# Output projection of layer 0 ended in passes over 256 and 320 tokens, with two tiles' norm beside the second pass

## What is computed

```python
def rms_norm(x, w):
    y = xf * lax.rsqrt(jnp.mean(xf * xf, axis=-1, keepdims=True) + NORM_EPS)
    return (y * w.astype(jnp.float32)).astype(x.dtype)

def diff_attn_output(o, g, subln_w, w_out):
    of = head_rms_norm(o) * subln_w * (1.0 - LAMBDA_INIT)
    gated = of.reshape(b, s, DA_WIDTH) * jax.nn.silu(g)
    return gated @ w_out

for layer in range(DEPTH):
    hp = rms_norm(y_prompt, norm_pre)
    ...
    y_prompt = y_prompt + rms_norm(diff_attn_output(op, gp, ...), norm_post)
```

## Time and profile before

| | |
|---|---|
| time, 3 runs | 3826.13, **3837.47** (median), 3842.16 us |
| profiled execution, its own time | 3831.26 us |
| its span and mean granted clock | 3828.5 us, 0.993 |
| PE busy | 3709.1 us (97%), 26980 matmuls |
| DVE, ACT, POOL busy | 1453.5 (38%), 1123.9 (29%), 150.6 (4%) us |
| DMA queue of loads | 565.92 MB, 47.6% of 16 engines' span |
| chain that ended last | PE 50%, then DVE 2%, each other 1% or less |

### The profile page before, as it was taken

The page is one execution under the profiler, slowest core; times in us unless marked ns, Lnnn a source line. Parts: engine busy times, 40 slices in busy tenths (PEclk is TensorE's granted clock), DMA queues, the critical chain, the costliest instruction groups (busy, mean ns, idle before and its releaser), DMA issues.

```text
span 3828.5 us, 70107 instructions
## 1 busy us (share of the span) xinstructions
PE 3709.1 (97%) x26980; PEld 3275.7 (86%) x26980; DVE 1453.5 (38%) x2215; ACT 1123.9 (29%) x1808; POOL 150.6 (4%) x87
## 2 busy tenths in 40 slices
PE   7999999999999999989899999999999999999998
PEld 7987887888788877767898989999989899989998
DVE  4244334433443344323633333333333324243345
ACT  4233233323332333221422222222222222232223
POOL 1000000200020002002200000000000000000000
PEclk9999999999999999999999999999999999999999
DMA  5456778687768776764442525242424343443333
GB/s 172 151 177 188 239 239 237 212 244 236 238 210 245 238 237 215 244 197 168 135 139 83 165 83 166 79 164 85 160 86 161 94 149 98 163 138 130 108 122 121
DMA packets 472204, 642.91 MB, mean 168 GB/s; under 512 B 35649, under 2 KB 294850, under 8 KB 468738
## 3 DMA queue, kind: packets, MB, share of 16 engines
q1 hardware_dynamic: 407122, 565.92, 47.6%
q10 hardware_dynamic: 64336, 72.24, 5.6%
q0 software_dynamic: 416, 0.28, 0.1%
HBM read 566.09 MB, written 70.65 MB: 166 GB/s over the span
## 4 chain that ended last, share of the span: by engine, by line
PE 50%; DVE 2%; issue 1%; DMA 1%; ACT 1%; POOL 1%; SPq 1%; ACTq 0%; DVEq 0%; POOLq 0%
PE low_banks L965 42%; PE high_banks L965 6%; PE high_banks L968 1%; DMA area<-in_cache_v 1%; POOL area L1897 1%; DVE WL L1523 0%; ACT WH L1236 0%; DMA WR<-in_w_in_ret 0%; SPq L900 0%; SPq L901 0%; ACTq L1401 0%; DVE area L1782 0%; ACT area L1236 0%; DVE area L1545 0%; ACTq L1400 0%
## 5 line engine op out<-in xcount | busy, mean ns | idle before, releaser
L965 PE MATMUL low_banks<-XH,WH 128*128 128x288 f32 (+2 forms) x6656 | 1545.6, 310 | 42.0 <-DVE XL L1528 16.6
L965 PE MATMUL low_banks<-XH,WL 128*128 128x288 f32 (+2 forms) x6656 | 1455.4, 296 | 0.0
L965 PE MATMUL low_banks<-XL,WH 128*128 128x288 f32 (+2 forms) x6656 | 1452.6, 296 | 0.0
L965 PEld LDWEIGHTS low_banks<-XH,WH 128*128 128x128 f32 x6656 | 1080.4, 190 | 142.4 <-issue 96.0
L965 PEld LDWEIGHTS low_banks<-XH,WL 128*128 128x128 f32 x6656 | 1083.7, 189 | 0.0
L965 PEld LDWEIGHTS low_banks<-XL,WH 128*128 128x128 f32 x6656 | 1083.4, 189 | 0.0
L1523 DVE TENSOR_TENSOR WL<-WR,WH 128x1024 fp32r<-128x1024 f32 x436 | 533.4, 1223 | 817.8 <-ACT WH L1236 812.7
L1236 ACT ACTIVATE WH<-WR 128x1024 fp32r<-128x1024 f32 x436 | 461.2, 1058 | 923.4 <-PE low_banks L965 652.6
L965 PE MATMUL high_banks<-area 128*32 128x512 f32 (+8 forms) x3696 | 654.1, 547 | 16.1 <-DVE area L1554 5.6
L1236 ACT ACTIVATE area<-high_banks 128x512 f32<-128x512 f32 x480 | 270.2, 569 | 1139.4 <-PE high_banks L968 756.8
L968 PEld LDWEIGHTS high_banks<-eye_sb,area 128*128 128x128 f32 (+2 forms) x3080 | 352.4, 142 | 156.6 <-issue 116.8
(11 more groups left out here) (113 smaller groups left out, 840.9 us busy)
## 6 DMA issues: line engine op xcount, KB each, us to landing
area<-in_cache_k SPq DMA_DIRECT2D x512, 256.0 KB, 4.1
area<-in_cache_v SPq DMA_DIRECT2D x512, 256.0 KB, 4.1
WR<-in_w_in_ret SPq DMA_DIRECT2D x200, 512.0 KB, 3.5
WR<-in_w_in_attn SPq DMA_DIRECT2D x136, 512.0 KB, 5.4
out<-area ACTq DMA_DIRECT2D x73, 512.0 KB, 3.1
WR<-in_w_out_ret SPq DMA_DIRECT2D x68, 512.0 KB, 3.3
area<-in_state_ret SPq DMA_DIRECT2D x64, 512.0 KB, 5.6
WR<-in_w_out_attn SPq DMA_DIRECT2D x32, 512.0 KB, 5.5
```

The costliest lines, as they stand in the source:

```text
L965: return nc.tensor.matmul(out, a, b, start=start, stop=stop, skip_group_check=True)
```

## The change

It does five things.

1. The last four of the eight column groups in the last part of the output projection (steps 4 to 7) are done twice, first over tokens 0 to 256, then over 256 to 576; 64 tiles become 96, 32 of them full.
2. `y_sq` now also scales yT by the post weight (two ACT copies, line L1245 of the new file), and stands ahead of tile 2 and the weight split behind it, where it stood behind both. `y_turn` (transpositions) takes the place of `y_tr`; the diagonal goes.
3. Token tiles 0 and 1 are summed, squared, scaled and turned beside the 320-token pass (numbers 70 to 95 in `early`); tiles 2 to 4 beside layer 1's first 64 tiles (`finish`). All scales are on DVE; POOL's multiplication goes.
4. The splits of the gated output for `kt` 12 to 15 go from slots 120 to 129 to 208, 214, 220, 226.
5. `sample_sq` becomes four small matmuls and a power over 64x2, and a new stage `sample_rs` (DVE two products with the identity, PE one matmul, DVE one copy) spreads the result. They stand at slots 3 and 12 of the next half, and in the tail ahead of the 24 tiles and behind the seventh; gate and `split_s` behind the tenth.

```diff
-        if h % 2:
-            put(127, Stage("sample_sq"))
...
-            mine = merge(mine, {20: [Stage("sample_gate", pair=(h - 3) // 2)], 22: [Stage("store_sample", pair=(h - 3) // 2)]})
+            mine = merge(mine, {3: [Stage("sample_sq")], 12: [Stage("sample_rs")], 20: [Stage("sample_gate", pair=(h - 3) // 2)],
+                                22: [Stage("store_sample", pair=(h - 3) // 2)]})
...
-        at = merge(at, {108 + 3 * k: [split_gated_attention(2 + k // 4, 8 + k)]})
+        at = merge(at, {(108 + 3 * k if k < 4 else 184 + 6 * k): [split_gated_attention(2 + k // 4, 8 + k)]})
...
+    out.append(Stage("sample_sq"))
     for n in range(24):
         out += proj.tile()
-    out.append(Stage("sample_gate", pair=pairs - 1))
-    out += [Stage("split_s", kt=12 + k, k=k) for k in range(4)]
+        if n == 6:
+            out.append(Stage("sample_rs"))
+        if n == 9:
+            out.append(Stage("sample_gate", pair=pairs - 1))
+            out += [Stage("split_s", kt=12 + k, k=k) for k in range(4)]
     out.append(Stage("relay_loads"))
+    between = NormBetween()
     loads = norm_loads(1)
-    for n in range(64):
-        out += proj.tile()
+    for n in range(96):
+        out += between.early(n) + proj.tile()
         if n % 8 == 3 and loads:
             out.append(loads.pop(0))
-        if n % 8 == 2 and n > 8:
-            out.append(Stage("y_sq", s=n // 8 - 1))
     assert not loads
-    out.append(Stage("y_sq", s=7))
-    return out
+    return out, between
...
+class NormBetween(Norm):
+
+    def __init__(self):
+        super().__init__(1)
+        self.turns, self.groups = {}, {}
+        self.squares = {s: Stage("y_sq", s=s, layer=0, scaled=True) for s in range(4)}
+        for k, (lo, hi) in enumerate(((0, EARLY), (EARLY, T))):
+            self.squares.update({4 * (k + 1) + n: Stage("y_sq", s=4 + n, layer=0, lo=lo, hi=hi, scaled=True) for n in range(4)})
+
+    def group(self, tiles, after, freed):
+        out = Stage("y_group", tiles=tiles, after=after, freed=freed)
+        self.groups.update({t: out for t in tiles})
+        return [out]
+
+    def sum_y(self, t, freed):
+        group = self.groups[t]
+        self.turns[t] = Stage("y_turn", t=t, wide=True, after=group.a["after"], freed=freed)
+        self.y[t] = Stage("y_sum", t=t, wide=True, turn=self.turns[t], rstd=group, left=int(4 in group.a["tiles"] and t < 4))
+        return [self.turns[t], self.y[t]]
+
+    def spread(self, t, freed):
+        self.tr[t] = Stage("x_tr", t=t, in_low=False, after=self.scaled[t], freed=freed)
+        return [self.tr[t]]
+
+    def early(self, n):
+        if n % 8 == 2 and n > 8:
+            return [self.squares[n // 8 - 1]]
+        return {70: lambda: self.group((0, 1), self.squares[7], None), 73: lambda: self.sum_y(0, self.groups[0]),
+                76: lambda: self.square(0), 79: lambda: self.sum_y(1, self.y[0]), 81: lambda: self.scale(0), 83: lambda: self.square(1),
+                86: lambda: self.store(0), 87: lambda: self.scale(1), 88: lambda: self.spread(0, self.y[1]),
+                95: lambda: self.spread(1, self.tr[0])}.get(n, lambda: [])()
+
+    def finish(self, proj):
+        out = [self.squares[11]]
+        at = {2: lambda: self.store(1), 10: lambda: self.group((2, 3, 4), self.squares[11], self.tr[1]),
+              14: lambda: self.sum_y(2, self.groups[2]), 18: lambda: self.square(2), 21: lambda: self.sum_y(3, self.y[2]),
+              25: lambda: self.scale(2) + self.square(3), 28: lambda: self.spread(2, self.y[3]), 30: lambda: self.store(2),
+              34: lambda: self.sum_y(4, self.tr[2]), 36: lambda: self.scale(3) + self.square(4), 42: lambda: self.spread(3, self.y[4]),
+              44: lambda: self.store(3), 46: lambda: self.scale(4), 48: lambda: self.store(4), 53: lambda: self.spread(4, self.tr[3])}
+        for t in range(2 * 32):
+            out += at[t]() if t in at else []
+            out += proj.tile()
+        return out
...
-        for s in range(8):
-            proj.step("out0", s * 256, rows[2 + part:3 + part], xs[8 + 4 * part:12 + 4 * part], kind="+", hh=s, layer=0)
+        order = [(s, None) for s in range(8)]
+        if part:
+            order[4:8] = [(s, (s % 2, lo, hi)) for lo, hi in ((0, EARLY), (EARLY, T)) for s in range(4, 8)]
+        for s, span in order:
+            proj.step("out0", s * 256, rows[2 + part:3 + part], xs[8 + 4 * part:12 + 4 * part], span=span, kind="+", hh=s, layer=0)
...
-                mm(bank[4][:, 0:256], ones, oQ[:].rearrange("p a b -> p (a b)")).then_inc(sem["full4"], 1)
+                for h in range(2):
+                    for e in range(2):
+                        last = mm(bank[4][0:SMP, 2 * h:2 * h + 2], oQ[:, 2 * h + e, :], ones[:, 0:2], start=e == 0, stop=e == 1)
+                last.then_inc(sem["full4"], 1)
+
+            def sample_rs(g):
+                pe.wait_ge(sem["sd_ready"], c.done("sd_ready"))
+                free(4)
+                mm(bank[4][:, 0:128], ones[0:SMP, :], sdiag[:]).then_inc(sem["full4"], 1)
...
-            def y_sq(g, s, lo=0, hi=T, scaled=False):
+            def y_sq(g, s, layer, lo=0, hi=T, scaled=False):
                 for n in ("proj0_drained", "proj1_drained", "y_acc"):
                     act.wait_ge(sem[n], c.before(n))
                 nc.scalar.activation(ysq[:, :, lo:hi], yT[:, 2 * s:2 * s + 2, lo:hi], ACT.Square).then_inc(sem["y_sq"], 1)
                 if scaled:
                     act.wait_ge(sem["y_sq"], c.done("y_sq"))
-                    o.link(copy(yT[:, 2 * s, lo:hi], yT[:, 2 * s, lo:hi], scale=post[:, 1, 2 * s:2 * s + 1]))
-                    copy(yT[:, 2 * s + 1, lo:hi], yT[:, 2 * s + 1, lo:hi], scale=post[:, 1, 2 * s + 1:2 * s + 2]).then_inc(sem["y_scaled"], 1)
+                    o.link(copy(yT[:, 2 * s, lo:hi], yT[:, 2 * s, lo:hi], scale=post[:, layer, 2 * s:2 * s + 1]))
+                    copy(yT[:, 2 * s + 1, lo:hi], yT[:, 2 * s + 1, lo:hi], scale=post[:, layer, 2 * s + 1:2 * s + 2]).then_inc(sem["y_scaled"], 1)
...
-                o.link(v.tensor_reduce(rsS[:].rearrange("p (h q) -> p h q", h=2),
-                                       bank[4][:, 0:256].rearrange("p (h e q) -> p h q e", h=2, e=2), AX.X, ADD))
-                variance(rsS[:], 256).then_inc(sem["drained4"], 1)
+                sums = bank[4][0:SMP, 0:4].rearrange("p (h n) -> p h n", n=2)[:, :, 0]
+                v.tensor_scalar(rs2[:, 0:2], sums, 1.0 / 256, EPS, MUL, ADD).then_inc(sem["drained4"], 1)
+
+            def sample_rs(g):
+                dve.wait_ge(sem["s_rstd"], c.before("s_rstd"))
+                for n in ("pv_done", "drained5"):
+                    dve.wait_ge(sem[n], c.before(n))
+                o.link(v.tensor_scalar(sdiag[:, 0:SMP], ident[0:SMP, 0:SMP], rs2[:, 2:3], None, MUL))
+                v.tensor_scalar(sdiag[:, SMP:2 * SMP], ident[0:SMP, 0:SMP], rs2[:, 3:4], None, MUL).then_inc(sem["sd_ready"], 1)
+                dve.wait_ge(sem["full4"], c.done("full4"))
+                v.tensor_copy(rsS[:], bank[4][:, 0:128]).then_inc(sem["drained4"], 1)
...
-                rsqrt(rsS[:], rsS[:], "s_rstd", n=128)
+                rsqrt(rs2[:, 2:4], rs2[:, 0:2], "s_rstd", R=SMP, n=2)
```

158 lines of the change are left out of this document (39 added, 119 removed).

## The result

Twelve runs of each kernel: before 3839.57 us median (3826.13 to 3843.12), after **3851.32** (3838.32 to 3857.45), ratio 1.0035 with a 95% interval of 1.0025 to 1.0044. The change costs some 13 us, 0.35%, inside the 0.5% band and on the slower side, as forecast (+7). The profiled executions lie further apart (3831.26 and 3854.09), since before's was one of its quickest; so the traces say where the time went, and the medians how much it was.

What follows compares the result with a forecast made beforehand. The kernel was taken as a stream of TensorE tiles with few holes. Terms -9 - 7 + 9 + 13 = +6, with rounding +7 us, gave 3844.5 us on the median of 3837.47; range 3822 to 3866.

Steps and rivals of the forecast that it cites:

- Part A: Output splits leaving slots 120 to 129: waits of 5.34 and 1.58 us and 2.4 us of clock go, gain 9 us.
- Part B: Last sample gate: the small power ends the 4.68 us wait and 2.6 to 2.8 us clock loss, gain 7 us.
- Part C: Other three gates moved to slots 3 and 12: new waits at three boundaries, net 9 us lost, bounds -4 and +14.
- I count 4: Last boundary: of the old 4.39 us wait before the squares' matmul, 4 us counted as gained.
- rival 2: Half clock follows short holes in Part D's stretch and at Part C's boundaries: +20, 3857.5 us; chance 0.22.
- Part D: Stretch from last sample gate to layer 1's first full-width step: net +13 us, bounds -16 and +25.
- 256 steps: Narrow 256-token steps: ScalarE work ahead of the weight split leaves holes, three total 6.1, plus a first 3.5; together 9.7 us.
- 320 steps: 320-token steps: small holes 1.4, wait behind tile 0's transposition 6.9, first transposition's wait 1.5; 9.8 us in all.
- layer 1's first steps: Three token tiles finished beside layer 1's start instead of two: holes 6.8 x 2.25 = 15 us.
- I count two more: Part D's clock: two more low-clock spells, 3.4 us, less 1.4 lost at the old sums, net 2 us.
- The first (waits covered): Rival: VectorE fills gaps and copies hide, so Part C and Part D turn to gains: -36, 3801 us; chance 0.15.
- The third: Rival that the gates do not cost: Part C is -4, Part D as forecast, -7 in all, 3830.5 us; chance 0.06.

Runs made afterwards that it cites:

- a_only: Kernel before with only the output splits for kt 12 to 15 moved to slots 208 to 226; ratio 0.9959, 15.7 us below before.
- own17: Kernel before with Part A and Part B, squares at slot 127, spreading at slot 17, diagonal in its own buffer; ratio 0.9961, 15.0 us below before.
- abc: Kernel before with Part A, Part B and Part C, the seam between layers left as before; ratio 0.9995, 1.9 us below before.
- fill_d: Changed kernel with unused filler matmuls ahead of waits at steps 40, 48, 56, 64 and 88 of the last 96 tiles; ratio 1.0024, 9.2 us above before.
- turn: ab2 with transpositions replacing the diagonal's fp32 matmuls in the old seam, scaled copies behind the weight split; ratio 0.9967, 12.7 us below before.
- best: turn with own17's slots for squares and spreading; ratio 0.9965, 13.4 us below before.
- ab2: Kernel before with Part A and Part B, first three pairs' squares at slot 127 in small form, spreading at slot 12; ratio 0.9985, 5.8 us below before.
- fill: abc with nine unused fp32 matmuls of ones on TensorE ahead of the wait for the sample squares; ratio 0.9975, 9.6 us below before.

## Why the prediction was right, and which terms were off

- **Right:** the sign, the size within the range, and the waits in each part. +7 was forecast, +13 came. Of the signs named ahead, the two old waits are gone, the boundary waits are there, and the hole behind the first transposition is 7.05, a little over its 5 to 7. Two came out less well: TensorE's idle from the last gate on is 30.3 for 37, and the clock of that stretch is 0.90, or 0.89 with the gate's own work, at the very bound that was named as a sign of being wrong.
- **Part A, -9:** -9.0 in after's profile, -7.9 in a_only's. The medians say -16 with an interval of 5; the 9 is what the traces show, the medians' interval (11 to 21) leaves it out, and that surplus stays open.
- **Part B, -7:** the wait of 4.68 went. The clock's 2.6 did not go in full: after too ran at half clock behind the small matmuls (1767 to 1773, 0.50), as before did in part. The stretch gives 3.4 to 5. By the medians A and B together are 15 (own17), forecast 16; that the sum is so near is luck, since A alone measured 16 and B nothing that the medians resolve.
- **Part C, +9:** the two waits were sized right. Two things were not. "I count 4" for the old wait at the third boundary was too good, since in its place TensorE waits 2.9 for the output's low halves (1480 in after). And no half clock was counted in the sum of C; rival 2 had priced it. It came behind some waits and not behind others: C cost 10.5 in abc's profile, 18.8 in after's, and its place 13 by the medians of abc and own17.
- **Part D, +13:** +15 by the medians of after and abc, +18 by the stretch in their two profiles. Work -9.4 (forecast -10). Holes: full-width steps 0.62 (still among the 24 tiles), 1.03, 0.59, 0.61 = 2.9 (2.5); 256 steps 3.04, none, 1.60, 1.97 = 6.6 (9.7), the missing one because the half clock stretched the step that should have waited; 320 steps 1.52 + 7.05 = 8.6 (9.8); layer 1's first steps 12.8 (15). The step that failed is **"I count two more"** of the clock: +2 was forecast, some 14 of full speed was lost, of which fill_d puts 7 (its profile) or 4 (its medians, not told from nothing) as a cost beside the holes.
- **Sums.** Three of the prediction's sums don't come out. The chain between full-width steps, given as 6.4, adds up to 5.9 from its own terms; with 5.9 the first narrow step's hole is 3.0 in place of 3.5, and 3.04 was measured. The lower bound of -16 for D doesn't follow from "holes no longer than before", which gives -8. And rival 2 with C's upper bound is 3862.5, not 3866.
- **Rivals.** The first (waits covered) fell: each predicted wait is in the trace. The second, half clock, came true in its mechanism, behind four or more holes of D and at boundaries, but at half its price, because much of the slow time covers waits that were there anyway. So the forecast's holes were too long and its clock too good, and the two errors offset each other: that D came within 2 us of the forecast is luck in this part. The third fell with C.
- **The rule on transpositions** (the Trainium skill, "TensorE: Matmul & The Clock Gate", "Part 4: PE-mode transpose"). turn and best put transpositions in place of matmuls and their stretch's clock is 0.92 to 0.93 where ab2 and own17 have 0.96 and 0.95. That agrees with the rule in direction, but the holes grew as well, so no run here separates the two. The section "A second HAM failure mode: psum-queue depth-cycling" of the same page of the Trainium skill has micro-idles between groups of matmuls and a cost beside the idle itself. This case agrees in kind: 0.59 over 4 us behind the 2.16 us wait in after, and 1.00 where fill fills it.

## What to carry to other kernels

The version to keep is before with parts A and B, squares at slot 127 and spreading at slot 17 (own17): 15 us below before, 28 below after. Before an operation is moved, list what stands ahead of it on the engine that must feed it, not only on the engine that waits: both slot 3 and the narrow steps failed by one weight split or one pair of copies ahead in a queue. When steps are cut narrower, the fixed work for each step must fit in the shorter cover; here a chain of 4.9 us, by the prediction's estimate, stood beside 2.9 us of tiles, and TensorE waited 1.6 to 2.0. And a hole of 2 us on TensorE may cost a second time by the clock, but in a place where TensorE waits again soon, that cost is partly the same wait; price it by a run with filler matmuls.
